# Mixer of a two-block kernel: projection groups as three float32r passes, convolution groups and a modulation unit on ScalarE and GpSimd, another order of loads

## The reference, cut to what matters

```python
mod = silu(c) @ w_ada[l] + b_ada[l]                 # six vectors of 1024: 8 loaded units of 768 columns
h = rms_norm(x, g) * (1 + sc1) + sh1
proj = h @ w_in[l]                                  # 1024 x 3584: 14 groups of 256 columns
v = proj[a] * sigmoid(proj[g])                      # 512 channels
v = causal depthwise conv, 31 taps, + conv_b
y_a = silu(layer_norm(v)) @ w_conv_out + b_conv_out
y_b = (window means of proj[pool] - proj[pool]) @ pool_w * pool_scale
x = x + g1 * ((sigmoid(gate_a) * y_a + sigmoid(gate_b) * y_b) @ w_out[l])
```

## Time and profile before

| what | value |
|---|---|
| median of three runs | 2016.56 us (2015.21 to 2021.18) |
| profiled execution | 2018.86 us |
| its span, first to last instruction | 2017.0 us |
| mean granted clock of TensorE | 0.976 |
| TensorE busy | 1937.6 us, 96% |
| VectorE busy | 1289.5 us, 64% |
| ScalarE busy | 735.5 us, 36% |
| GpSimd busy | 70.3 us, 3% |

### The profile page before, as it was taken

One profiled execution on the slowest core, in us unless ns is written; L12 is line 12 of the kernel. 1 busy time (PEld: TensorE's weight loads), 2 busy tenths in 40 slices (PEclk: granted clock), 3 DMA queues, 4 the chain that ended last, 5 costly groups with the idle time before them and its releaser, 6 DMA issues.

```text
span 2017.0 us, 29866 instructions
## 1 busy us (share of the span) xinstructions
PE 1937.6 (96%) x11691; PEld 1547.6 (77%) x11691; DVE 1289.5 (64%) x2018; ACT 735.5 (36%) x1248; POOL 70.3 (3%) x111
## 2 busy tenths in 40 slices
PE   7999899998999899998999999999999999999998
PEld 7888645555888645545999887899989998878887
DVE  5999423435998324335788757666668887575555
ACT  2021222223021222224433556544464436555445
POOL 0101000000201000000000002000000000110000
PEclk6999799999999799999999999999999999999999
DMA  9859899997858799998599842677638996526651
GB/s 352 306 167 326 320 414 406 406 419 272 290 177 314 312 408 402 418 413 300 209 328 349 272 126 84 231 247 254 216 126 292 327 349 158 147 75 205 202 189 40
DMA packets 266958, 546.99 MB, mean 271 GB/s; under 512 B 31042, under 2 KB 187212, under 8 KB 242252
## 3 DMA queue, kind: packets, MB, share of 16 engines
q1 hardware_dynamic: 266828, 545.19, 74.7%
HBM read 544.08 MB, written 4.22 MB: 272 GB/s over the span
## 4 chain that ended last, share of the span: by engine, by line
PE 70%; DVE 18%; issue 4%; ACT 4%; SPq 2%; DMA 1%; POOL 1%; DVEq 0%; ACTq 0%; POOLq 0%
PE ps L859 11%; PE ps L783 10%; PE ps L709 8%; DVE acc L2083 6%; PE ps L960 6%; PE ps L740 4%; PE ps L742 4%; PE ps L741 4%; PE ps L811 3%; PE ps L770 3%; DVE arena L2217 3%; DVE wsp L2138 2%; PE ps L772 2%; PE ps L926 2%; SPq L444 2%
## 5 line engine op out<-in xcount | busy, mean ns | idle before, releaser
L2138 DVE TENSOR_TENSOR wsp<-ring,wsp 128x1024 fp32r<-128x1024 f32 x264 | 321.5, 1223 | 173.6 <-ACT wsp L1625 166.8
L1625 ACT ACTIVATE wsp<-ring 128x1024 fp32r<-128x1024 f32 x264 | 277.9, 1056 | 322.7 <-PE ps L742 196.1
L740 PE MATMUL ps<-hsp,wsp 128*128 128x256 f32 x1120 | 319.6, 285 | 5.0 <-DVE hsp L2613 3.0
L741 PE MATMUL ps<-hsp,wsp 128*128 128x256 f32 x1120 | 316.9, 283 | 0.0
L742 PE MATMUL ps<-hsp,wsp 128*128 128x256 f32 x1120 | 316.8, 283 | 0.0
L709 PE MATMUL ps<-arena,ring 128*128 128x256 f32 x1280 | 283.0, 381 | 4.1 <-PE ps L709 2.7
L709 PEld LDWEIGHTS ps<-arena,ring 128*128 128x128 f32 x1280 | 242.8, 191 | 39.0 <-issue 5.0
L783 PE MATMUL ps<-wsp,asp 128*128 128x512 f32 x1056 | 255.4, 394 | 1.6 <-DVE wsp L2138 0.2
L859 PE MATMUL ps<-ring,hpick 128*64 128x512 f32 x1024 | 230.5, 603 | 8.1 <-issue 8.1
L783 PEld LDWEIGHTS ps<-wsp,asp 128*128 128x128 f32 x1056 | 194.1, 188 | 50.1 <-DVE wsp L2138 9.7
L740 PEld LDWEIGHTS ps<-hsp,wsp 128*128 128x128 f32 x1120 | 214.8, 192 | 7.7 <-DVE wsp L2138 3.6
(11 more groups left out here) (280 smaller groups left out, 2778.3 us busy)
## 6 DMA issues: line engine op xcount, KB each, us to landing
ring<-in_w_expert_gate_dram SPq DMA_DIRECT2D x64, 1024.0 KB, 8.8
ring<-in_w_expert_up_dram SPq DMA_DIRECT2D x64, 1024.0 KB, 11.1
ring<-in_w_expert_down_dram SPq DMA_DIRECT2D x64, 1024.0 KB, 10.3
ring<-in_ada_w_dram SPq DMA_DIRECT2D x48, 1152.0 KB, 9.3
ring<-in_ffn_w_gate_dram SPq DMA_DIRECT2D x44, 1024.0 KB, 11.8
ring<-in_ffn_w_up_dram SPq DMA_DIRECT2D x44, 1024.0 KB, 13.9
ring<-in_ffn_w_down_dram SPq DMA_DIRECT2D x44, 1024.0 KB, 5.2
ring<-in_w_ada_dram SPq DMA_DIRECT2D x32, 1152.0 KB, 12.0
```

The costliest lines, as they stand in the source:

```text
L740: mm(dst, hi, v_hi, start=start, stop=False, skip_group_check=True)
L741: mm(dst, hi, v_lo, start=False, stop=False, skip_group_check=True)
L1625: act_(split_part(at % SPLITS, 0, n), piece(unit, n), ACT.Identity).then_inc(S.whi, 1)
L2138: v_.tensor_tensor(split_part(at % SPLITS, 1, n), piece(unit, n), split_part(at % SPLITS, 0, n, F32), ALU.subtract).then_inc(S.wlo, 1)
```

## The change

- From the third group on, a projection group is three float32r passes. ScalarE rounds each of the 24 weight pieces of 128x1024 into one of four buffers (`high_win`), VectorE leaves the remainder in place of the weights (`low_win`). The hidden state is split the same way in two halves. The first two groups stay in fp32.
- Convolution groups 1 and 3 leave VectorE: ScalarE scales the 31 shifted inputs, two taps at a time (`weigh_taps`), and GpSimd adds the pairs. Groups 0 and 2 stay on VectorE, cut into pieces between the remainders.
- Modulation unit 5 leaves VectorE: ScalarE weighs its eight chunks in place (`weigh_unit`), GpSimd adds them into the first, TensorE sums that over the partitions.
- The sums over the convolution stand behind groups 12 and 13 instead of 11 and 12, the sum of unit 4 behind group 8, that of unit 7 behind the second output group. VectorE weighs unit 6 in two parts and unit 7 ahead of the ga products.
- Loads are reordered, and units are released by ScalarE instead of TensorE, in the mixer and at three places of the attention.

```diff
+            sp.wait_ge(bias_w, 1)
+            sp.dma_start(scratch, bias_rows).then_inc(bias_r, 16)
             for l in range(L):
                 group_unit(0, l, WIN_1[0], a.w_in, WIN_GROUPS[0])
                 lc = bass.ds(l, 1)
                 ada_unit(0, l, a.w_ada, 3)
+                group_unit(0, l, WIN_1[1], a.w_in, WIN_GROUPS[1])
                 ada_unit(0, l, a.w_ada, 4)
-                for u in (1, 2):
-                    group_unit(0, l, WIN_1[u], a.w_in, WIN_GROUPS[u])
-                if l == 0:
-
-                    sp.wait_ge(bias_w, 1)
-                    sp.dma_start(scratch, bias_rows).then_inc(bias_r, 16)
+                group_unit(0, l, WIN_1[2], a.w_in, WIN_GROUPS[2])
                 ada_unit(0, l, a.w_ada, 5)
...
-                for u in (3, 4):
-                    group_unit(0, l, WIN_1[u], a.w_in, WIN_GROUPS[u])
+                group_unit(0, l, WIN_1[3], a.w_in, WIN_GROUPS[3])
+                ada_unit(0, l, a.w_ada, 6)
+                group_unit(0, l, WIN_1[4], a.w_in, WIN_GROUPS[4])
...
+                group_unit(0, l, OUT_1[0], a.w_out, [0, 1, 2])
                 ada_unit(0, l, a.w_ada, 7)
-                group_unit(0, l, OUT_1[0], a.w_out, [0, 1, 2])
                 ahead_unit(l, 0)
+                group_unit(0, l, OUT_1[1], a.w_out, [3])
                 ahead_unit(l, 1)
-                group_unit(0, l, OUT_1[1], a.w_out, [3])
                 ahead_unit(l, 2)
...
+                    def pass_of(c, w, v, start=False, stop=False):
+
+                        for k in range(KD):
+                            done = mm(ps[:, i % 4, c * T:(c + 1) * T], w[:, k, :], v[:, k, :],
+                                      start=(start and k == 0), stop=(stop and k == KD - 1), skip_group_check=True)
+                        return done
                     for c in range(2):
+                        p = 2 * (i - 2) + c
                         if i == 0 and c == 0:
                             for k in range(KD):
                                 pe.wait_ge(S.h, k + 1)
...
+                        elif i == 2:
+                            if c == 0:
+                                pe.wait_ge(S.hhi, 2)
+                            pe.wait_ge(S.rhi, p + 1)
+                            pass_of(c, mix_hi[:, p % HIGHS], hm_hi, start=(c == 0))
+                            pe.wait_ge(S.rlo, p + 1)
+                            pass_of(c, win_piece(p, ring_lo), hm_hi)
+                        elif i > 2:
+                            pe.wait_ge(S.rhi, p + 1)
+                            pass_of(c, mix_hi[:, p % HIGHS], hm_hi, start=True)
+                            pass_of(c, mix_hi[:, p % HIGHS], hm_lo).then_inc(S.rused, 1)
+                            pe.wait_ge(S.rlo, p + 1)
+                            last = pass_of(c, win_piece(p, ring_lo), hm_hi, stop=True)
                         else:
...
-                    last.then_inc(S.proj, 1)
-                    if g == 2 or i == 13:
-                        pe.wait_ge(S.proj, i + 1)
-                        release(pe, unit)
                     if i == 2:
+                        pe.wait_ge(S.hlo, 2)
+                        for c in range(2):
+                            last = pass_of(c, mix_hi[:, c], hm_lo, stop=True)
+                            if c == 0:
+                                last.then_inc(S.rused, 1)
+                        last.then_inc(S.rused, 1)
+                        pe.wait_ge(S.rused, 2)
+                        pe.sem_inc(S.proj, 1)
+                    else:
+                        last.then_inc(S.proj, 1)
+                    if i == 3:
                         ada_later(3, 5, 1)
-                    elif i == 3:
+                    elif i == 8:
                         ada_later(4, 4, 1)
...
+                    elif i == 12:
...
                         for c in range(KC):
-                            pe.wait_ge(S.conv, c + 1)
+                            if c % 2 == 0:
+                                pe.wait_ge(S.conv, c // 2 + 1)
+                            else:
+                                pe.wait_ge(S.conv_p, c // 2 + 1)
                             last = mm(ps[:, 6, 0:T], ones[:], cv[:, c, :], start=(c == 0), stop=(c == KC - 1))
                         last.then_inc(S.ln1, 1)
...
-                    elif i == 12:
...
-                ada_later(5, 5, units_in(3))
...
-                ada_later(6, 4, units_in(4))
+                pe.wait_ge(S.ada_mod, units_in(3))
+                pe.wait_ge(S.pada, PADA)
+                for c in range(AC):
+                    last = mm(ps[:, 5, c:c + 1], wada(ADA_1[5])[:, 0, c * P:(c + 1) * P], ones[:, 0:1],
+                              start=True, stop=True)
+                last.then_inc(S.ada_sum, 1)
...
-                pe.wait_ge(S.ya_t, 4)
-                release(pe, BRANCH_1)
-                ada_later(7, 4, units_in(6))
-                pe.wait_ge(S.mix, 4)
+                ada_later(6, 4, units_in(4))
+                def mixed(k):
+
+                    if j == 0 and c == 0 and k % 2 == 0:
+                        pe.wait_ge(S.mix, k // 2 + 1)
+                    return ga[:, k, :]
...
-                    if j >= 2:
-                        pe.wait_ge(S.o_t, j + 1)
-                        release(pe, unit)
                     if j == 1:
+                        ada_later(7, 4, units_in(6))
+                    elif j == 2:
                         ahead_later(0)
...
-                    pe.wait_ge(A.mm, 1)
-                    release(pe, M0)
...
+                def used(s, count, unit):
+
+                    eng.wait_ge(s, count)
+                    release(eng, unit)
+
+                def high_win(p):
+
+                    u, g = divmod(p // 2 + 2, 3)
+                    if p % 2 == 0 and g != 1:
+                        wait_landed(eng, 0, l, WIN_1[u], parts=(g // 2,))
+                    if p // 2 + 2 == 13:
+                        wait_landed(eng, 0, l, WIN_1[u], parts=(1,))
+                    if p >= HIGHS:
+                        eng.wait_ge(S.rused, p - HIGHS + 1)
+                        eng.wait_ge(S.rlo, p - HIGHS + 1)
+                    act_(mix_hi[:, p % HIGHS], win_piece(p, ring), ACT.Identity).then_inc(S.rhi, 1)
+
+                def weigh_taps(n, *pairs):
+
+                    c, sums = 2 * n + 1, TAPS // 2 + 1
+                    for m in pairs:
+                        if m == 0:
+                            eng.wait_ge(S.v, n + 1)
+                            if n:
+                                eng.wait_ge(S.tap_add, sums)
+                        elif m >= 4:
+                            eng.wait_ge(S.tap_add, sums * n + m - 3)
+                        for t in range(min(2, TAPS - 2 * m)):
+                            j = 2 * m + t
+                            last = act_(tap_pair(m)[:, t, :], vpad[:, c, j:j + T], ACT.Identity,
+                                        scale=vB[:, j * KC + c:j * KC + c + 1],
+                                        bias=row(vA, ROWS_1, "conv_b", c) if j == 0 else 0.0)
+                        last.then_inc(S.tap, 1)
...
+                    eng.wait_ge(S.proj, i + 1)
+                    if i in (8, 11, 13):
+                        release(eng, WIN_1[(8, 11, 13).index(i) + 2])
...
+                def weigh_unit(k0, k1):
+
+                    w = wada(ADA_1[5])
+                    for k in range(k0, k1):
+                        if k == 0:
+                            wait_landed(eng, 0, l, ADA_1[5], parts=(0,))
+                        elif k == 6:
+                            wait_landed(eng, 0, l, ADA_1[5], parts=(1,))
+                        act_(w[:, k, :], w[:, k, :], ACT.Identity, scale=cvec[:, k:k + 1]).then_inc(S.pada_x, 1)
...
+                for p in range(4):
+                    high_win(p)
+                for q in range(2):
+                    eng.wait_ge(S.h, 4 * q + 4)
+                    act_(hm_hi[:, 4 * q:4 * q + 4, :], h[:, 4 * q:4 * q + 4, :], ACT.Identity).then_inc(S.hhi, 1)
+                glu_gate(0)
+                weigh_taps(0, 0, 1)
+                high_win(4)
+                weigh_taps(0, 2)
+                high_win(5)
+                used(S.proj, 3, WIN_1[0])
+                weigh_taps(0, 3, 4)
+                high_win(6)
+                weigh_taps(0, 5)
+                glu_gate(1)
+                high_win(7)
+                weigh_taps(0, 6, 7)
+                high_win(8)
+                weigh_taps(0, 8)
...
+                high_win(22)
+                weigh_taps(1, 14, 15)
+                gate(11)
+                high_win(23)
+                weigh_unit(0, 6)
+                for i in (12, 13):
+                    gate(i)
+                    if i == 12:
+                        weigh_unit(6, KD)
                         for c in range(KC):
                             eng.wait_ge(S.lnc, c + 1)
                             act_(sg[:, c, :], cv[:, c, :], ACT.Square).then_inc(S.lnq, 1)
+                    else:
```

(89 more changed lines are left out.)

120 lines of the change are left out of this document (89 added, 31 removed).

## The result

The changed kernel takes 2106.24 us (median of four runs, 2104.42 to 2108.23), the kernel before 2015.88 beside it (2015.15 to 2021.18): a ratio of 1.044, 95% interval 1.042 to 1.046. It is slower, by 90 us. The profiled execution has a span of 2102.7 us, 85.7 more than before.

The account below looks back on a forecast made before the run. VectorE's queue was taken to set T, the end of the mixer's convolution, with TensorE just beside it. Terms of 36.2 us (layer 0) and 35.6 (layer 1) gave +71.8 on the median 2016.56: 2088.4 us, range 2034 to 2122.

Parts of the forecast that it names:

- VectorE without a hole from 60 to 172: Sign in the changed profile, layer 0: VectorE runs without idle time from about 60 to 172 us.
- late start: VectorE's first modulation unit waits for remainders of the second weight unit: 6.4 us lost in layer 0, 5.8 in layer 1.
- Own work: VectorE up to the convolution's end: two convolution groups leave (-32.1), remainders come (+30.2 and +2.5), sum +0.6 us a layer.
- Adds: GpSimd's adds for two convolution groups hold up VectorE: 24 us a layer, 22.5 to 26.2.
- Unit sums: GpSimd's seven sums of 128x768 for the modulation unit, close to the convolution's end, cost VectorE 4 us (0 to 7.5).
- Tail: From the convolution's end to the last update of x: -4.8 to the output projection, +6 behind, net +1.2 us.
- Rival (a): GpSimd's adds cost VectorE little, 0 to 0.38 us each, falling into unseen waits: 2032 to 2057 us; chance 0.15.
- Rival (b): TensorE, not VectorE, sets the end, so the change is faster: 1992 us; chance 0.08.
- Rival (c): TensorE's granted clock falls to its lower level through the projection: +18 us a layer, 2124 us; chance 0.07.
- Rival (d): Full blocking: every GpSimd instruction costs VectorE its whole duration, 51 instead of 28 us a layer, 2134 us; chance 0.05.

Follow-up runs that it names:

- run 3: The changed kernel with VectorE's first modulation unit moved ahead of the remainders of pieces 2 and 3; 2093.9 us (ratio 1.037).
- thin adds: The changed kernel, but GpSimd adds only the first 8 of 256 columns of each pair of taps; 2041.0 us (ratio 1.011).
- run 2: The kernel before with extra GpSimd sums in each layer on an unused buffer: 28 of 128x512, 2064.5 us; 14 of 128x1024, 2077.3 us.

## Why the prediction was right, and where its sizes were off

Forecast were 2088.4 us and +71.8; measured are 2106.2 and +90 (profiled +85.7). The mechanism held: VectorE sets T, and what the change gives it is worth less than what it costs. By its steps, layer 0:

- **VectorE without a hole from 60 to 172.** It starts at 60.16 (forecast 59.9) and has no hole over 0.8 us until 179.0. The late start, forecast at 6.4 and 5.8, was worth 8.3 and 5.3 at T (run 3).
- **Own work +0.6.** With thin adds T is 6.1 us later than before (143.2 against 137.1), where late start and own work gave 7.0. These 6.1 contain the hole of 3.59 us that only the kernels with thin adds have, and some loss to window sums and thin adds, so own work is some microseconds below the term; a remainder starts 1.13 after its forerunner where I had counted 1.26.
- **Adds 24 (22.5 to 26.2).** 25.5 by taking them out, 0.85 for one by itself, where the price taken from one modulation step was 0.88. That 24 fits so well is in part luck: in the change the adds kept VectorE busy 29.8 us longer, about 1.0 for a long one, and 4.5 of that are taken back by waits for ScalarE that came up only without them.
- **Unit sums 4 (0 to 7.5).** This is the term that failed: 10.3 and 10.1, outside its bounds. I put half of them behind T and priced the rest at 0.59 per us. All seven fell ahead of T, and the price was taken from the window sums, which have many short instructions. A long one costs all but 0.44 us of its time: with the 1.83 us that the prediction estimated for it, 7 x (1.83 - 0.44) = 9.7.
- **Tail +1.2 (-4.8 to +6.5).** T to the output projection took 37.6 us, against 39.8 before and 35 forecast; unit 7 landed for a start at T+26.8 instead of T+24.5, and the sums behind T ran at the lower clock. From there to the last update 37.3 (forecast 36 to 37), to the second norm 40.0 against 34.5. The tail is -2.2 + 5.6 = +3.4; layer 1: +2.2.

So 36.2 became 45.3 by -0.9 (start and own work), +1.5 (adds), +6.3 (unit sums), +2.2 (tail). Rival (a) is out: an add costs 0.85 to 1.0, not 0 to 0.38. Rival (b) needed every add to be free; with VectorE freed of both kinds of sums TensorE does wait less, but the kernel stays 1% above the one before. Rival (c): the clock did fall, to 0.83 in the stage, but VectorE sets the end there, and behind T it is worth 3 to 4 us. Rival (d) is too dear, by about 0.44 us an instruction in run 2: 35.8 us of layer 0 came back at T without adds and unit sums, where it gave 51 and the forecast 28. Counted by the instruction, 35 sums of 0.44 us less take its 51 down to 35.6.

The Trainium skill, "SBUF — State Buffer", section "SBUF: two separate sides", says that whichever of the two engines starts first holds the port pair for its whole instruction and the other blocks fully. The two runs with added sums agree with a loss per instruction rather than a shared bandwidth, but show 0.85 of 1.27 and 1.96 of 2.40 us lost; the measurement decides.

What stays open: why 0.44 us of each sum are free; why an add held VectorE up for about 1.0 us in the change and for 0.85 in run 2; and how large the gain of the releases in the attention is, which is below the scatter of that part.

## What to carry to other kernels

Work that goes from VectorE to GpSimd can come back as waiting. In the two runs with added sums each long GpSimd sum beside a two-input VectorE operation cost VectorE the sum's own duration less about 0.4 us. In the change the adds cost 25.5 us at T against the 32.1 of taps that VectorE gave up, and only 3.9 were gained. Where it falls counts as much: seven sums cost 10 us a layer ahead of the point that VectorE sets, and 2 to 3.5 behind it. Shortening TensorE where VectorE ends last bought only a longer wait here, and the granted clock behind that wait was lower.

## What was not expected of the hardware

- GpSimd's sums of 128x512 and 128x1024 cost VectorE 0.85 and 1.96 us each in run 2: about 0.43 us is free at both lengths, so fewer and longer instructions cost more for the same columns (2077 against 2064 us).
- Behind one wait of 5.14 us at T the next fp32 group took 9.02 us at a granted clock of 0.78, a mean between the levels of 1.2 and 2.4 GHz; behind one of 0.91 it took 7.07 at 1.00. In layer 1 one wait of 2.15 us came ahead of a group of 8.76.
- Both sides slow down: GpSimd's sum of 128x512 took 1.69 us beside VectorE, 1.27 alone; that of 128x1024 2.94 beside it, 2.40 alone.
